# Scan stage: skip coefficients unit by unit, first loads ahead of the bulk, first gate by columns

## The reference, cut to what matters

```python
lmat = jnp.einsum("bcign,bcjgn->bcijg", cm, bm)[..., None] * decay
y_diag = jnp.einsum("bcijgr,bcjgrp->bcigrp", lmat, xdt)
...
y_off = jnp.einsum("bcign,bcigr,bcgrpn->bcigrp", cm, jnp.exp(a_cum), s_prev)
...
y = y + d_skip.astype(jnp.float32)[:, None] * xs.astype(jnp.float32)
y = y.reshape(b, L, D_INNER) * jax.nn.silu(z.astype(jnp.float32))
```

## Time and profile before

| | |
|---|---|
| median of 3 runs | 2603.93 us (2603.7 to 2607.3) |
| profiled execution, its own time | 2605.13 us |
| its span | 2603.4 us |
| mean granted TensorE clock | 0.949 |
| TensorE / VectorE / ScalarE / GpSimd busy, whole span | 91% / 65% / 44% / 19% |
| the scan stage | from 1030.25 us (first transfer issued) to 1228.9 us (first matmul of attention) |

### The profile page before, as it was taken

The page is one execution under the profiler, slowest core; times in us unless marked ns, Lnnn a source line. Parts: engine busy times, 40 slices in busy tenths (PEclk is TensorE's granted clock), DMA queues, the critical chain, the costliest instruction groups (busy, mean ns, idle before and its releaser), DMA issues. The chain is left out here.

```text
span 2603.4 us, 34473 instructions
## 1 busy us (share of the span) xinstructions
PE 2381.5 (91%) x13468; PEld 1964.2 (75%) x13468; DVE 1695.9 (65%) x1900; ACT 1139.1 (44%) x1538; POOL 492.3 (19%) x425
## 2 busy tenths in 40 slices
PE   7899999999999997898999799997963999999992
PEld 2788888887798877565777599997753788888882
DVE  5555555535315762676777667655556899999996
ACT  3333333221123111354677644433332777777772
POOL 0000000222002440597010000002323011101112
PEclk9899999999999999799999899998876999999996
DMA  6222234877525784998221498894326899999994
GB/s 227 61 83 75 78 107 113 190 215 261 174 99 186 271 300 150 299 295 282 77 88 42 127 265 254 237 268 142 125 102 272 310 402 406 404 398 396 396 363 145
DMA packets 325417, 565.21 MB, mean 217 GB/s; under 512 B 21813, under 2 KB 232773, under 8 KB 301401
## 3 DMA queue, kind: packets, MB, share of 16 engines
q1 hardware_dynamic: 298890, 459.00, 51.4%
q0 software_dynamic: 23856, 99.20, 12.6%
q10 hardware_dynamic: 2528, 5.06, 0.6%
HBM read 451.69 MB, written 106.26 MB: 214 GB/s over the span
## 5 line engine op out<-in xcount | busy, mean ns | idle before, releaser
L2629 DVE TENSOR_TENSOR e_wlo<-e_w,e_whi 128x2048 fp32r<-128x2048 f32 x188 | 425.6, 2290 | 41.9 <-ACT e_whi L2578 40.5
L2578 ACT CAST e_whi<-e_w 128x2048 fp32r<-128x2048 f32 x192 | 365.4, 1909 | 123.5 <-PE e_gu L2755 82.3
L452 PE MATMUL f_lat<-h_hi,w_hi 128*128 128x512 f32 x800 | 253.8, 398 | 9.0 <-DVE w_lo L603 9.0
L452 PE MATMUL f_lat<-h_lo,w_hi 128*128 128x512 f32 x800 | 251.3, 395 | 0.0
L452 PE MATMUL f_lat<-h_hi,w_lo 128*128 128x512 f32 x800 | 251.2, 395 | 0.0
L2089 PE MATMUL b_acc<-b_hi,b_whi 128*128 128x256 f32 x768 | 218.8, 285 | 7.9 <-issue 7.9
L2089 PE MATMUL b_acc<-b_lo,b_whi 128*128 128x256 f32 x768 | 218.1, 284 | 0.0
L2089 PE MATMUL b_acc<-b_hi,b_wlo 128*128 128x256 f32 x768 | 218.1, 284 | 0.0
L452 PEld LDWEIGHTS f_lat<-h_hi,w_hi 128*128 128x128 f32 x800 | 137.9, 189 | 39.4 <-DVE w_lo L603 10.0
L452 PEld LDWEIGHTS f_lat<-h_hi,w_lo 128*128 128x128 f32 x800 | 140.1, 188 | 29.7
L452 PEld LDWEIGHTS f_lat<-h_lo,w_hi 128*128 128x128 f32 x800 | 140.1, 188 | 29.6
(11 more groups left out here) (368 smaller groups left out, 5406.9 us busy)
## 6 DMA issues: line engine op xcount, KB each, us to landing
e_w<-in_w_gate_up SPq DMA_DIRECT2D x128, 1024.0 KB, 11.6
e_w<-in_w_down SPq DMA_DIRECT2D x64, 1024.0 KB, 9.7
w_raw<-in_w_in SPq DMA_DIRECT2D x50, 512.0 KB, 4.1
t_space<-xbcT POOLq DMA_DIRECT2D x18, 1280.0 KB, 6.4
before<-t_space SPq DMA_DIRECT2D x16, 1024.0 KB, 4.5
shared<-before SPq DMA_DIRECT2D x64, 256.0 KB, 6.8
l_w<-in_w_ssd_br SPq DMA_DIRECT2D x20, 768.0 KB, 6.8
xbcT<-t_out POOLq DMA_DIRECT2D x20, 640.0 KB, 4.4
```

The source lines that it names most:

```text
L452: mm = nc.tensor.matmul(o, weights[:, b, k, :], part[:, k, a:a + n], start=(k == 0 and n_pass == 0), stop=(k == KT - 1 and n_pass == 2))
L2578: nc.scalar.copy(whi[:, slot % SPLIT], w[:, slot]).then_inc(w_hi, 1)
L2629: V.tensor_tensor(wlo[:, slot % SPLIT], w[:, slot], whi[:, slot % SPLIT].bitcast(F32), ALU.subtract).then_inc(w_split, 1)
```

## The change

Own rows of chunk 0 are issued by SP ahead of everything (before: by ACT). For chunk 0 the gate is loaded in four pieces of 512 columns with the groups, and counts into the group's semaphore. Behind group 0 of chunk 0, SP waits for the own rows, both constants and the first two row buffers before it issues the rest. Coefficients are made for one unit at a time, behind that unit's weighing: one reduction of one diagonal and one instruction that multiplies and adds for 8 heads. The gate products of a chunk wait for all four coefficients of the chunk before. The three memsets of ones stand together at the start of VectorE's list.

```diff
@@ -1271,6 +1271,9 @@
         def where(u):
             return u // G, u % G, (u // G) % NB
 
+        def group_count(n, g):
+            return (48 if g else 64) * (n // NB + 1) + (16 if n % NB == 0 else 0)
+
         def load_own(eng, n):
             j = n % NB
             for part_, (src, lane) in enumerate(((cumrow, 0), (cumrow, 1), (logrow, 0), (logrow, 1))):
@@ -1288,6 +1291,8 @@
                         sp.wait_ge(y_made, G * (n - NB + 1))
                         sp.sem_inc(carrier, 1)
                     at = slice(CTX + n * P, CTX + n * P + P)
+                    if n == 0:
+                        load_own(sp, 0)
                     sp.dma_start(bc[j].rearrange("p a g q -> p (a g q)"), bcF[n]).then_inc(bc_in[j], 16)
                     if n:
                         load_own(sp, n)
@@ -1297,7 +1302,15 @@
                         sp.dma_start(x[j][:, cols], xbcT[at, cols]).then_inc(group_in[j][g], 16)
                         for d in range(2):
                             sp.dma_start(before_t[j][:, d, cols], before[d, n, :, cols]).then_inc(group_in[j][g], 16)
-                    sp.dma_start(z[j], zT[n * P:n * P + P, :]).then_inc(z_in[j], 16)
+                        if n == 0:
+                            sp.dma_start(z[0][:, cols], zT[0:P, cols]).then_inc(group_in[0][g], 16)
+                            if g == 0:
+                                sp.wait_ge(cum_in[0], 64)
+                                sp.wait_ge(const_in, 32)
+                                for k in range(2):
+                                    sp.wait_ge(rows_in[k], 48)
+                    if n:
+                        sp.dma_start(z[j], zT[n * P:n * P + P, :]).then_inc(z_in[j], 16)
 
                 def store(u):
                     n, g, _ = where(u)
@@ -1323,7 +1336,7 @@
                     pe.wait_ge(bc_in[j], 16 * (n // NB) + 16)
                     if n >= 1:
                         pe.wait_ge(w_made, G * n)
-                        pe.wait_ge(coef_made, n)
+                        pe.wait_ge(coef_made, G * n)
                     for k in range(G):
                         mm = nc.tensor.matmul(g_ps[:, k, :], bc[j][:, 0, k, :], bc[j][:, 1, k, :], start=True, stop=True)
                     mm.then_inc(g_made, 1)
@@ -1348,7 +1361,7 @@
                     if u >= 1:
                         pe.wait_ge(front_read, u)
                         pe.wait_ge(back_read, u)
-                    pe.wait_ge(group_in[j][g], (48 if g else 64) * (n // NB + 1))
+                    pe.wait_ge(group_in[j][g], group_count(n, g))
                     for d in range(2):
                         mm = nc.tensor.matmul(off_ps[:, d], bc[j][:, 1, g, :], before_t[j][:, d, 512 * g:512 * g + 512], start=True, stop=True)
                     mm.then_inc(off_made, 1)
@@ -1408,7 +1421,6 @@
                     act.dma_start(all_cum[2:ROWS, j].rearrange("r d h i -> r (d h i)").bitcast(F32), s.lanes).then_inc(rows_in[j], 16)
                     load_rows(j)
                     if j == 0:
-                        load_own(act, 0)
                         act.dma_start(sq[:], s.squares.rearrange("p (a q) -> p a q", q=P)[:, 0:3, :]).then_inc(const_in, 16)
                         act.dma_start(dskip[:], s.x["d_skip"].to_broadcast([P, HEADS])).then_inc(const_in, 16)
                 exponentials(0)
@@ -1426,21 +1438,17 @@
                         dve.wait_ge(args_made, HALVES * u + half + 1)
                         V.copy_predicated(arg_ps[:, half, 0], above, arg_ps[:, half, 1]).then_inc(merged, 1)
 
-                def coefficients(n):
-                    j = n % NB
-                    dve.wait_ge(g_made, n + 1)
-                    for g in range(G):
-                        V.tensor_tensor_reduce(gdump[:], g_ps[:, g, :], diagonal[:], 1.0, NEG, ALU.add, ALU.max,
-                                               gdiag[:, g:g + 1]).then_inc(coef_step, 1)
-                        dve.wait_ge(coef_step, (G + 1) * n + g + 1)
+                def coefficients(u):
+                    n, g, j = where(u)
+                    if g == 0:
+                        dve.wait_ge(g_made, n + 1)
+                        dve.wait_ge(group_in[j][0], group_count(n, 0))
+                    V.tensor_tensor_reduce(gdump[:], g_ps[:, g, :], diagonal[:], 1.0, NEG, ALU.add, ALU.max, gdiag[:, g:g + 1]).then_inc(coef_step, 1)
                     if n >= 2:
-                        dve.wait_ge(skip_made, G * (n - 1))
-                    dve.wait_ge(group_in[j][0], 64 * (n // NB) + 64)
-                    cof = coef[:, n % 2].rearrange("p (g h) -> p g h", g=G)
-                    V.tensor_tensor(cof, tab[:, j, DT, 0].rearrange("p (g h) -> p g h", g=G),
-                                    gdiag[:].unsqueeze(2).to_broadcast([P, G, HPG]), ALU.mult).then_inc(coef_step, 1)
-                    dve.wait_ge(coef_step, (G + 1) * n + G + 1)
-                    V.tensor_tensor(coef[:, n % 2], coef[:, n % 2], dskip[:], ALU.add).then_inc(coef_made, 1)
+                        dve.wait_ge(skip_made, G * (n - 2) + g + 1)
+                    dve.wait_ge(coef_step, u + 1)
+                    h = slice(HPG * g, HPG * g + HPG)
+                    V.scalar_tensor_tensor(coef[:, n % 2, h], tab[:, j, DT, 0, h], gdiag[:, g:g + 1], dskip[:, h], ALU.mult, ALU.add).then_inc(coef_made, 1)
 
                 def weigh(u):
                     n, g, j = where(u)
@@ -1463,24 +1471,22 @@
                         dve.wait_ge(sum_step, 2 * (u - 2) + 2)
                     V.tensor_tensor(pre[:, u % 2], diag_ps[:], skip[:, u % 2], ALU.add).then_inc(diag_read, 1)
 
-                V.memset(own_cum[0][ONES].bitcast(F32), 1.0).then_inc(own_ones, 1)
+                for j in range(NB):
+                    V.memset(own_cum[j][ONES].bitcast(F32), 1.0).then_inc(own_ones, 1)
                 dve.wait_ge(const_in, 32)
                 V.tensor_scalar(diagonal[:], sq[:, 0, :], -NEG, NEG, ALU.mult, ALU.add).then_inc(diag_made_const, 1)
                 dve.wait_ge(diag_made_const, 1)
                 merge(0)
                 coefficients(0)
                 weigh(0)
-                for j in range(1, NB):
-                    V.memset(own_cum[j][ONES].bitcast(F32), 1.0).then_inc(own_ones, 1)
                 for u in range(UNITS):
                     if u + 1 < UNITS:
                         n, g, j = where(u + 1)
                         merge(u + 1)
                     scale_front(u)
                     if u + 1 < UNITS:
-                        if g == 0:
-                            coefficients(n)
                         weigh(u + 1)
+                        coefficients(u + 1)
                     add_inside(u)
                 u, n, g, j = UNITS - 1, LCHUNK - 1, G - 1, (LCHUNK - 1) % NB
                 b = u % 2
@@ -1491,7 +1497,7 @@
                 dve.wait_ge(diag_read, UNITS)
                 V.tensor_tensor(pre[:, b], pre[:, b], part[:, b, 0], ALU.add).then_inc(y_last, 1)
                 dve.wait_ge(y_last, 2)
-                dve.wait_ge(z_in[j], 16 * (n // NB) + 16)
+                dve.wait_ge(z_in[j], 16 * (n // NB + (j > 0)))
                 dve.wait_ge(y_out[g], 16 * n)
                 V.tensor_tensor(y[:, g], pre[:, b], z[j][:, 512 * g:512 * g + 512], ALU.mult).then_inc(y_last, 1)
 
@@ -1499,9 +1505,8 @@
             def _(pool):
                 def skipped(u):
                     n, g, j = where(u)
-                    if g == 0:
-                        pool.wait_ge(coef_made, n + 1)
-                    pool.wait_ge(group_in[j][g], (48 if g else 64) * (n // NB + 1))
+                    pool.wait_ge(coef_made, u + 1)
+                    pool.wait_ge(group_in[j][g], group_count(n, g))
                     if u >= 2:
                         pool.wait_ge(diag_read, u - 1)
                     nc.gpsimd.tensor_tensor(heads(skip[:, u % 2]), heads(x[j][:, 512 * g:512 * g + 512]),
...
```

More of the change, by code:

```diff
@@ L1396, in scale_back @@
                     if g == 0:
-                        act.wait_ge(group_in[j][0], 64 * (n // NB) + 64)
+                        act.wait_ge(group_in[j][0], group_count(n, 0))
                     act.wait_ge(off_made, u + 1)
@@ L1523, in finish @@
                     pool.wait_ge(sum_step, 2 * u + 2)
-                    if g == 0:
-                        pool.wait_ge(z_in[j], 16 * (n // NB) + 16)
+                    if g == 0 and n:
+                        pool.wait_ge(z_in[j], 16 * (n // NB + (j > 0)))
                     if n >= 1:
```

## The result

| | before | changed |
|---|---|---|
| median of 5 runs | 2606.86 us (2603.7 to 2610.63) | 2625.66 us (2622.17 to 2629.89) |
| ratio, 95% interval | | 1.007, 1.0056 to 1.0085 |
| profiled execution, its span | 2605.13, 2603.4 us | 2629.8, 2628.1 us |
| mean granted TensorE clock | 0.949 | 0.941 |
| first matmul of attention | 1228.90 us | 1251.97 us |

The three runs of the table ahead of the prediction are among the five of before. Two executions stand outside all ratios here, both of the kernel under "The gate products later" (10741.7 and 4055.2 us); one of them is its profiled one, so no row of that kernel is used.

A forecast was written before the change was run, and what follows sets the result against it. TensorE was taken as the steady bound, GpSimd a near second, the store queue limiting the start. Terms: -9.5 (start) + 2 (clock) + 1.8 (coefficients) = -5.7 us: 2599.4 profiled, 2598.2 median, range 2593.5 to 2605.5.

The forecast's parts named there:

- (4): At chunk ends, gate products also wait for the last unit's coefficients: 0.31 us more per chunk, +1.8 us in all.
- (3): At GpSimd's unit 4, TensorE is held 1.8 us; a half-clock spell costs at most 6.6, taken as 2.
- (1): Start of the stage: group 0 lands at 1044.0, chunk 1's gate products come at 1065.0, 11.3 us earlier.
- (2): Bulk loads wait on SyncE's queue: store 0 lands at 1086.2 and sets GpSimd's unit 4; TensorE 9.5 us earlier.
- rival (a): Busiest four transfer engines set store 0, at 1091.3, whatever the order: -0.6 us, 2603.3; chance 0.25.
- Rival (c): Late store 0, at 1093.3, and a hold that drops the clock for one 6.2 us spell: +5.6, 2609.5; chance 0.08.
- the one on the period from chunk 1's gate products to chunk 2's: Sign on TensorE: a period well over 24.7 us means hold or clock cost more than the 1.8 and 2 taken.
- The gap before the gate products: Sign in steady chunks: TensorE's gap there would be near 0.66 us instead of 0.23.

The follow-up runs named there:

- The gate products later: Changed kernel with the next chunk's gate products moved behind the state products of the chunk's last unit: 2607.53 us, ratio 0.9989 to the kernel before.

## Why the prediction was wrong

**The failed step is (4), the size of the small product.** I took 0.19 us and bounded it by 0.38, from two rows of products on 32 columns of SBUF. Those two stood in the block ahead of the weighing, and I did not look what GpSimd was doing beside them. It was doing nothing: its next instruction was waiting for these very products. In the trace of before, 15 of the 16 such products ran beside an idle GpSimd and took 0.19; the one that did not took 0.33 and ended with GpSimd's. That is the first pair of rows here, GpSimd and VectorE; the last is GpSimd's, waiting behind the products that I took the price from:

```profile
1163.57 1.28 POOL L1528 TENSOR_TENSOR l_wo<-y_total,l_wo 128x512 f32<-128x512 f32 x1
```
```profile
1164.57 0.33 DVE L1440 TENSOR_TENSOR y_coef<-y_tab,y_gdiag 128x32 f32<-128x32 f32 x1
```
```profile
1103.47 1.04 POOL L1507 TENSOR_TENSOR y_skip<-shared,y_coef 128x512 f32<-128x512 f32 x1 [0.51 <-DVE y_coef L1443]
```

So the price was taken at the one place where the instruction can't meet its neighbour. In its new place, at the chunk's end, GpSimd has its back-to-back products of 1.26 us, and the product measured up to 1.31. So the gap was 0.74 to 2.24 in place of at most 0.85. I named the term as a loss in every chunk, and put it at 0.31 a chunk. With it went the second error: I gave a clock price only to the one hold of (3), none to a gap that comes in each chunk. The gaps of 1.4 to 2.2 us had spells of 7 to 17 us at 0.50 behind most of them, and the chunks 3 to 5 took 4.4 to 9.4 us more than 20.53. Over six periods that is +33.5 us, of which 16.1 also stand in the kernel with the old coefficients (hold and its cold clock, 139.4 against 123.33) and 17.4 come from the coefficients. For these I had +1.8.

**(1) came out, in part by luck.** Exponents at 1040.37 (forecast: near 1040), VectorE's constant at 1038.66 (1041), first state product at 1045.99 (1044), gate products of chunk 1 at 1062.56 (1065). The data came 2 us later than forecast, and the first chunk made up for it: 16.57 us from state product to gate products, where I had 21.0. Most of it ran at a clock of 0.98, and this I had not foreseen: before, the clock was 0.50 from 1060.7 to 1073.9. Of the lead of 13.3 us, 6.9 are the earlier data and 6.4 the shorter first chunk; how much of the latter is the clock and how much the memsets isn't told apart.

**(2) had the right place and the wrong size.** It named store 0 as the next limit, and GpSimd's unit 4 as who waits. I said the store would land at 1086.2; it landed at 1090.3. On this point rival (a) was right: the last gate piece of chunk 0 landed at 1056.8 (before 1057.5, forecast 1053.4), the gate load of chunk 2 at 1089.9 (before 1089.5 by the earlier trace rows). Counted from the stage's first transfer, store 0 landed 60.1 us in before, 60.5 in the changed kernel and 60.9 in the one with the old coefficients. That nothing comes sooner through a full queue I had as a rival at 0.25 and should have had as the forecast. (a)'s reason was not tested, the four busiest transfer engines; what the stores between the loads show is the order in the queue.

**(3) was far too small.** I put the hold at 1.8 us and its clock at 2. The slack was larger than my 4.0 us, and the path another one: not VectorE's scaling behind GpSimd's total, but its addition behind GpSimd's skip product, 6.9 us (9.95 less 3.05) in the changed kernel and 6.2 (13.80 less 7.60) with the old coefficients. And yet, with the old coefficients, the hold was 7.60, and with the clock behind it (0.64 for 25 us) it took 16.2 us, all of a lead of 14.1 and more. Rival (c) had the right mechanism, hold and cold clock, at its start, but at one spell of 6.2 us; it needed a late store for it. Here the store was on time, and TensorE had come too early for it. The lead turned into a wait of GpSimd (13.80 us), more than half of that into a hold of TensorE, and the hold then cost more than itself.

Of the ways that I named to find the prediction wrong, the one on the period from chunk 1's gate products to chunk 2's (well over 24.7) did not trip, at 24.15, but by chance: that period holds no hold, only the half clock behind the gap of 1.41, and the hold came a chunk later, in the 30.57. The gap before the gate products did trip.

## What to carry to other kernels

Price a small VectorE instruction by the neighbour it will have: one that reads tensors of SBUF alone can take as long as the GpSimd instruction beside it. Let TensorE wait for the instruction that frees its buffer, not for the last of a group, or move its work to where the wait is long over. Before an early start is paid for, look for the next thing that must come in time (here a store behind three chunks of loads) and move that first: the same start was worth 0 with the old queue and about 0.33% with stores between the loads. And compare two traces from the start of the stage, not of the span: of the 17.1 us by which chunk 1's gate products came earlier with the old coefficients, 3.0 were there before the stage began.

## What was not expected of the hardware

- An instruction of 8 elements a partition took 0.225 to 1.309 us, by what GpSimd did; with one of its tensors in PSUM 0.225 to 0.227.
- Gaps of 1.4 to 2.2 us in a TensorE that is else full were followed by 7 to 17 us at a granted clock of 0.50, though not each time: behind the 1.75 us at 1197 it stayed at 1.00. Behind gaps of 0.48 to 0.89 it stayed at 1.00 ten times of 14, in two kernels; four times it was at 0.50 for some 3 us. Such a short spell isn't the gap's for certain: the kernel with the old coefficients and without SyncE's wait has one too, at 1123, in a chunk with no gap over 0.23. Of the loss of 0.7% the shorter gaps and the clock together take away 0.6%.
- A TensorE with a lead of 14.1 us, counted from the stage's first transfer, was held 7.60 us and then ran at a mean clock of 0.64 for 25 us. Behind that it was 2.0 us later than without the lead.
